# Both matrices of an MLP in seven block products for eight, the first one completed before the second begins

## What is computed

```
def sq_relu_mlp(h, w1, w2):
    return jnp.square(jax.nn.relu(h @ w1)) @ w2
```

## Time and profile before

| | us |
|---|---|
| median of 3 runs | 1949.92 (1949.31 to 1952.12) |
| the profiled execution | 1952.2 |
| its span, first to last instruction | 1950.1 |
| PE busy | 1911.8 (98%), 8432 matmuls |
| DVE busy | 1542.7 (79%) |
| ACT busy | 819.8 (42%) |
| POOL busy | 575.8 (30%) |

### The profile page before, as it was taken

How to read it: one execution, slowest core, us unless ns; L and a number is a source line. 1 busy time by engine, 2 the same in 40 slices (tenths; PEclk the granted TensorE clock), 3 DMA queues, 4 the chain that set the end, 5 groups by cost and what they waited for, 6 DMA issues and landing times.

```text
span 1950.1 us, 22012 instructions
## 1 busy us (share of the span) xinstructions
PE 1911.8 (98%) x8432; PEld 1567.0 (80%) x8432; DVE 1542.7 (79%) x1677; ACT 819.8 (42%) x1011; POOL 575.8 (30%) x261
## 2 busy tenths in 40 slices
PE   7899999999999999999999999999999999999997
PEld 4678888878887878888888888888888888888886
DVE  7989999978898898768677686776867768677683
ACT  5455555553423344434334343343434434344343
POOL 0009999930000022322222222222222232222301
PEclk9999999999999999999999999999999999999998
DMA  9973222237797714222442224432244332342332
GB/s 389 401 273 109 100 94 95 99 149 292 299 408 281 295 67 172 102 97 102 150 151 100 98 98 147 145 114 97 98 139 146 109 108 97 135 152 103 109 130 86
DMA packets 83342, 308.87 MB, mean 158 GB/s; under 512 B 6705, under 2 KB 6961, under 8 KB 58673
## 3 DMA queue, kind: packets, MB, share of 16 engines
q1 hardware_dynamic: 83250, 307.64, 42.9%
HBM read 299.23 MB, written 8.39 MB: 158 GB/s over the span
## 4 chain that ended last, share of the span: by engine, by line
PE 84%; DVE 12%; issue 1%; ACT 1%; DMA 1%; SPq 1%; POOL 0%; POOLq 0%; DVEq 0%; ACTq 0%
PE ps L555 14%; PE ps L759 10%; PE ps L757 10%; PE ps L763 10%; PE ps L781 9%; PE ps L783 9%; PE ps L788 9%; PE ps L560 7%; DVE raw L1245 2%; DVE adar L1245 2%; DVE wlo L1267 2%; DVE ps L1341 1%; DMA raw<-w 1%; PE ps L821 1%; PE ps L822 1%
## 5 line engine op out<-in xcount | busy, mean ns | idle before, releaser
L1766 POOL TENSOR_TENSOR raw<-raw 128x1024 f32<-128x1024 f32 x116 | 315.3, 2718 | 1139.5 <-DVE wlo L1550 1136.1
L1550 DVE TENSOR_TENSOR wlo<-raw,whi 128x1024 fp32r<-128x1024 f32 x210 | 333.1, 1587 | 258.2 <-ACT whi L1108 258.0
L1108 ACT ACTIVATE whi<-raw 128x1024 fp32r<-128x1024 f32 x210 | 221.9, 1060 | 473.6 <-PE ps L763 327.7
L757 PE MATMUL ps<-hhi,whi 128*128 128x512 f32 x896 | 348.5, 389 | 0.0
L759 PE MATMUL ps<-hlo,whi 128*128 128x512 f32 x896 | 348.5, 389 | 0.0
L781 PE MATMUL ps<-whi,dhi 128*128 128x512 f32 x840 | 327.0, 389 | 1.5 <-DVE xb L1627 1.5
L783 PE MATMUL ps<-whi,dlo 128*128 128x512 f32 x840 | 326.8, 389 | 0.0
L555 PE MATMUL ps<-hlo,whi 128*128 128x512 f32 (+1 forms) x896 | 300.4, 390 | 7.1 <-DVE hlo L1251 7.1
L555 PE MATMUL ps<-hhi,whi 128*128 128x512 f32 (+1 forms) x896 | 301.2, 391 | 2.6 <-ACT hhi L1078 0.8
L1633 DVE TENSOR_TENSOR xb<-xb,ps 128x1024 f32<-128x1024 f32 x202 | 245.7, 1217 | 40.3 <-PE ps L788 40.3
L1341 DVE SCALAR_TENSOR_TENSOR ps<-xb,pr,ps 128x502 f32<-128x502 f32 (+22 forms) x358 | 230.8, 730 | 3.2 <-ACT ps L948 3.2
(11 more groups left out here) (192 smaller groups left out, 2122.1 us busy)
## 6 DMA issues: line engine op xcount, KB each, us to landing
raw<-w SPq DMA_DIRECT2D x112, 1024.0 KB, 6.7
raw<-w SPq DMA_DIRECT2D x128, 512.0 KB, 6.3
adar<-ada SPq DMA_DIRECT2D x36, 1024.0 KB, 7.4
raw<-ada SPq DMA_DIRECT2D x36, 1024.0 KB, 7.1
adaq<-ada SPq DMA_DIRECT2D x64, 256.0 KB, 3.3
xb<-xT SPq DMA_DIRECT2D x8, 1024.0 KB, 8.5
ada_h<-ada SPq DMA_DIRECT2D x4, 1024.0 KB, 17.9
ada_l<-ada SPq DMA_DIRECT2D x4, 1024.0 KB, 20.6
```

Source lines behind the costliest of these rows:

```text
L757: pe.matmul(ps[:, bank, :], tile, ch(hhi, 8 * h + k), start=h == 0 and k == 0, stop=False, skip_group_check=True)
L1550: dve.tensor_tensor(product_ring(wlo, n), quarter_tiles(g, OPERAND[i]), f(product_ring(whi, n)), ALU.subtract).then_inc(s_lo, 1)
L1766: pool.tensor_tensor(quarter(g, out), quarter(g, of), quarter(g, by), ALU.subtract).then_inc(t_done, 1)
```

## The change

**First matrix.** Tiles 0 to 7 stay as they are. Tiles 8 to 11 are made plainly (`direct_unit`, eight slots). Tiles 12 to 63 are made by 26 sets (`SETS`). A set is two row tiles of the hidden layer against the two halves of the channels and the two halves of the tokens: a 2 x 2 by 2 x 2 block product, in seven products (`product1`) of 24 matmuls whose moving operand has 256 columns (`HT`). The four sums of weight blocks of a set are made in place in `raw` by DVE (`sum1`), the four differences of `h` once, by POOL into `xb` and from there split into `t_upper` and `t_lower`. Three accumulators of a set leave PSUM on the way: `leave` on ACT copies three of them, and `c22`, `c12`, `c11` on DVE and `c21` on ACT make the four corners of the set.

**Forms.** All forms of 15 sub-blocks go through three staging buffers into a DRAM tensor (`fd`, `store_form` on SP), 105 of 512 KB each.

**Second matrix.** It begins when the first is complete. Its arithmetic is that of before, but two sub-blocks at a time are added in PSUM, in `GROUPS` (8): group 0 has one sub-block, groups 1 to 7 have two. So a half of the outputs of one group (`k`, `p`) has 14 slots and seven `take`s. The forms are read from DRAM into `hhi` and `hlo`, whose `h` is no longer needed, by DMAs that POOL issues (`load_form`, `load_sub`: 28 DMAs of 256 KB for a group), between its `term`s. The last sub-block is multiplied plainly as before, from forms in `hhi` and `hlo`.

**Smaller edits.** `x1` is parked in DRAM earlier; the last norm's input lies in other buffers (`fx`); `h2_hi` on ACT writes the full `h` first and then copies its high part; before the second product of the convolution PE warms up with 6 matmuls of 512 columns in place of 11 of 256; the order of PSUM banks at the end is another.

```diff
-PAIRS = 7
-GATES = (2, 2, 2, 2, 2, 3, 3)
 SUB = 4
 NSUB = FF // P // SUB
 HALF = U // 2
 RING = 4
 PROD = 7
 FORM = SUB // 2 * (T // 2)
-SLOTS_U = 2 * 2
-LAST_PAIR = 2 * NSUB - 3
-LAST_SLOTS = 2 * PROD + (LAST_PAIR - 1) * (SLOTS_U + PROD)
+HT = T // 2
+STAGES = 3
+DIRECT = 2 * SUB
+FIRST_SET = 3
+SETS = 2 * (NSUB - FIRST_SET)
+FORMS = (NSUB - 1) * PROD
+GROUPS = NSUB // 2
+W2 = DIRECT + SETS * PROD
+LAST_SLOTS = W2 + (NSUB - 1) * 2 * PROD
+GATE_AT = (1, 3, 5, 7, 10)
...
+        fd = nc.dram_tensor("forms", (FORMS, P, 2 * FORM), F32).ap()
...
+        WEIGHT1 = ((0, 0), (1, 0), (0, 0), (1, 0), (0, 0), (0, 1), (1, 1))
+        SUM1 = (None, 1, 2, 3, 4, None, None)
+        T_OF = (None, 1, 2, None, 3, None, 4)
+
+        def act1(x, k):
+
+            two, first = KC // 2 + k, bass.ds
+            if x in (0, 5, 3):
+                at = (two if x else k) * T + (HT if x == 3 else 0)
+                return hhi[:, first(at, HT)], hlo[:, first(at, HT)]
+            if x == 1:
+                return t_upper[:, k * HT:(k + 1) * HT], t_lower[:, k * T:k * T + HT]
+            if x == 2:
+                return t_upper[:, U + k * HT:U + (k + 1) * HT], t_lower[:, two * T + HT:two * T + T]
+            if x == 4:
+                return hhi[:, k * T + HT:k * T + T], t_lower[:, k * T + HT:k * T + T]
+            return hlo[:, k * T + HT:k * T + T], t_lower[:, two * T:two * T + HT]
...
+        MAKE = (2, 6, 5, 0, 3, 4, 1)
+        OF_SUM = {2: (0, 1), 5: (1, 2), 3: (0, 3), 1: (1, 4)}
+        PLAIN = {6: (1, 1), 0: (0, 0), 4: (0, 1)}
...
+            def store_form(n):
+
+                sp.wait_ge(form_lo, n + 1)
+                b, i = n // PROD, MAKE[n % PROD]
+                sp.dma_start(fd[b * PROD + i], stage(n % STAGES)).then_inc(form_out[n % STAGES], 16)
...
+            def product1(z, x):
+
+                n = slot1(z, x)
+                out = ps[:, bank1(z, (0, 2, 0, 2, 0, 1, 0)[x]), 0:HT]
+                fresh = x in (0, 1, 5)
                 pe.wait_ge(s_hi, n + 1)
...
+                if z == 0 and T_OF[x]:
+                    pe.wait_ge(t_lo, T_OF[x])
+                if x == 0:
+                    if z < 2:
+                        pe.wait_ge(tile_relu, (8, 12)[z])
+                    else:
+                        pe.wait_ge(c21_done, z - 1)
+                elif x == 1 and z >= 2:
+                    pe.wait_ge(c12_done, z - 1)
+                elif x == 5 and z >= 2:
+                    pe.wait_ge(c11_done, z - 1)
+                elif x == 2:
+                    pe.wait_ge(m1_out, z + 1)
+                elif x == 3:
+                    pe.wait_ge(m5_out, z + 1)
+                elif x == 4:
+                    pe.wait_ge(u2_out, z + 1)
+                elif x == 6:
+                    pe.wait_ge(c22_done, z + 1)
+                for k in range(8):
+                    tile = ring(whi, n)[:, k * P:(k + 1) * P]
+                    hi, lo = act1(x, k)
+                    pe.matmul(out, tile, hi, start=fresh and k == 0, stop=False, skip_group_check=True)
+                    pe.matmul(out, tile, lo, start=False, stop=False, skip_group_check=True)
+                pe.wait_ge(s_lo, n + 1)
+                for k in range(8):
+                    last = pe.matmul(out, ring(wlo, n)[:, k * P:(k + 1) * P], act1(x, k)[0], start=False, stop=False,
+                                     skip_group_check=True)
+                last.then_inc(s_mm, 1)
...
+            for v in range(SUB):
+                direct_unit(v)
+            for z in range(SETS):
+                for x in range(PROD):
+                    product1(z, x)
+            for k in range(GROUPS):
+                for p in range(2):
+                    for i in range(PROD):
+                        for a in range(subs(k)):
+                            product2(k, p, i, a)
...
+            def leave(z, kind, dest, n, done, x):
+
+                act.wait_ge(s_mm, slot1(z, x) + 1)
+                act.activation(small1(dest), ps[:, bank1(z, kind), 0:HT], ACT.Copy).then_inc(done, 1)
...
+            def sum1(z, n):
+
+                out, of, by = (((1, 0), (1, 0), (1, 1)), ((0, 0), (1, 0), (0, 0)),
+                               ((1, 0), (0, 1), (0, 0)), ((0, 0), (1, 1), (0, 0)))[n - 1]
+                if n == 1:
+                    dve.wait_ge(row_in[z % 2 * 2 + 1], 16 * (z // 2 + 1))
                 else:
...
+                    dve.wait_ge(s_sum, 4 * z + n - 1)
+                    dve.wait_ge(s_lo, slot1(z, n - 2) + 1)
+                dve.tensor_tensor(block1(z, *out), block1(z, *of), block1(z, *by), ALU.add if n == 1 else ALU.subtract
+                                   ).then_inc(s_sum, 1)
...
+            def c22(z):
+
+                b = z // 2 + 2
+                dve.wait_ge(m5_out, z + 1)
+                dve.wait_ge(s_mm, slot1(z, 4) + 1)
+                if z % 2 == 0:
+                    dve.wait_ge(form_lo, PROD * b + 2)
+                    dve.wait_ge(form_sum, 4 * b + 1)
+                dve.tensor_tensor(ch(hid, 2 + z % 2, HT, HT), ps[:, bank1(z, 0), 0:HT], small1(2), ALU.add
+                                  ).then_inc(c22_done, 1)
...
+            for z in range(SETS):
+                b = z // 2 + 2
+                for x in range(PROD):
+                    if x == 4:
+                        c22(z)
+                    if x == (3 if z % 2 else 6):
+                        c12(z)
+                    if z % 2 and x == 1:
+                        c11(z - 1)
+                    if z % 2 and x == 5:
+                        c11(z)
+                    ahead(z, x)
+                    if z == 0 and x == 0:
+                        t_low(4)
+                    if z % 2 == 0:
+                        if x == 0:
+                            form_add(b, 1)
+                        if x == 3:
+                            form_add(b, 2)
+                        if x == 4:
+                            form_add(b, 3)
+                        if x in (1, 2, 3, 5, 6):
+                            form_rest(PROD * b + (1, 2, 3, 5, 6).index(x))
+                    elif x == 0:
+                        form_add(b, 4)
+                        form_rest(PROD * b + 5)
+                    elif x == 2:
+                        form_rest(PROD * b + 6)
...
+            gate = 0
+            for k in range(GROUPS):
+                for p in range(2):
+                    for j in range(subs(k) * PROD):
+                        i, a = j // subs(k), j % subs(k)
+                        if a == subs(k) - 1:
+                            take(k, p, i)
+                        slot_lo(slot2(k, p, i, a) + RING)
...
-            for g in range(1, LAST_PAIR + 1):
-                for n in range(1, 5):
-                    term(g, n)
...
+            def load_form(k, i):
+
+                if k >= GROUPS:
+                    return
+                pool.wait_ge(s_mm, slot2(k - 1, 1, i, subs(k - 1) - 1) + 1)
+                for a in range(2):
+                    load_sub(2 * k - 1 + a, i, a)
+
+            for n in range(STAGES):
+                pool.wait_ge(form_out[n], 16 * 3)
+            for i in range(PROD):
+                if i in (0, 2, 4, 6):
+                    pool.wait_ge(s_mm, slot1(SETS - 1, (0, 3, 5, 6)[i // 2]) + 1)
+                load_sub(0, i, 0)
+            for k in range(GROUPS):
+                for p in range(2):
+                    for n in range(1, 5):
+                        for a in range(subs(k)):
+                            term(set_of(k, p, a), n, k, p, a)
+                        if p == 0 and k and n == 2:
+                            load_form(k, 5)
+                        if p == 0 and k and n == 3:
+                            load_form(k, 6)
+                        if p == 1 and n == 3:
+                            load_form(k + 1, 0)
+                            load_form(k + 1, 1)
+                    if p == 1:
+                        if k == 0:
+                            for n in range(STAGES):
+                                pool.wait_ge(form_out[n], 16 * (FORMS // STAGES))
+                        for i in (2, 3, 4):
+                            load_form(k + 1, i)
```

More of the change, by code:

```diff
@@ L111, in trunk_kernel @@
             ada_l = sb("ada_l", [P, 2, U], scope=first)
-        with ExitStack() as last:
-            xf = sb("xf", [P, KC * T], scope=last)
         hlo = sb("hlo", [P, KC * T], F32R)
@@ new lines, in t_parts, with bank1, stage @@
+        def t_parts(n):
+            src, low = (quadrants(buf[:])[:, (0, 1, 0, 1)[n - 1], :, (0, 1, 1, 0)[n - 1], :] for buf in (xb, t_lower))
+            if n < 3:
+                return src, t_upper[:, (n - 1) * U:n * U].rearrange("p (k n) -> p k n", n=HT), low
+            return src, quadrants((hhi if n == 3 else hlo)[:])[:, 0, :, 1, :], low
+        def bank1(z, kind):
+            return (0 if z % 2 else 4) + kind
+        def stage(n):
+            return wide[:, 2 * U + n * 2 * FORM:2 * U + (n + 1) * 2 * FORM]
@@ new lines, in _ @@
+            load_direct(2)
```

(58 more changed lines are left out.)

843 lines of the change are left out of this document (475 added, 368 removed).

## The result

The changed kernel takes 2021.09 us (median of 4 runs, 2019.85 to 2024.05) where the kernel before takes 1949.62: a ratio of 1.0366, 95% interval 1.0348 to 1.0384. It is slower by 3.7%, outside the range of 1880 to 2005. The profiled execution has a span of 2018.4 us, 68.3 more than before.

What follows compares the result with a forecast made beforehand. PE's matmuls were taken to set the time. Terms -70.7 + 12 + 1 + 4 + 2 + 28 = -23.7 took the profiled 1952.2 to 1928.5, less 2.3 for the median: 1926 us, 8-in-10 range 1880 to 2005.

Steps and rivals of the forecast that it cites:

- matmuls of the first matrix: PE in the sets: 4368 matmuls of 256 columns at 0.1133 us replace 2496 of 512 at 0.2266: -70.7 us.
- `c22` in even sets: First matrix: product 6 waits for `c22` on DVE 0.9 us, 13 times: +12 us (0 to 25).
- ahead of and in the first eight tiles: One more copy on ACT, 1.06 us, ahead of the MLP's first tile: +1 us (0 to 1).
- group 0, from the first matrix into the second: Between the matrices, POOL's first `term` comes behind loads waiting for PE's last product: +4 us (2 to 12).
- groups 1 to 7: Second matrix: 14 halves of 40.1 us, 2.0 over PE, as `term`s and DVE hinder each other: +28 us (0 to 70).
- last sub-block and tail: The last sub-block starts with forms just loaded: +2 us (0 to 5).
- the bound I had named: First matrix: 256-column matmuls at 0.120 us, 13 ns paid per matmul, making the matmul term -41 us.
- So I add up: 8 x 3.15 = 25.2 ...: Second matrix: eight `term`s, then remaining low parts, `take`s and gate parts, make a half 38.6 to 43.1 us; 40.1 taken.
- SP's 0.86 makes 37.2, just under PE: Second matrix: POOL's `term`s plus 14 load issues at SP's price of 0.86 us stay under PE's 38.1 per half.
- rival two: POOL's queue bounds the second matrix, deciding if an issue costs above 1.06 us; about 2011 us at 1.5; chance 0.23.
- Small edits: Extra ACT copy +1 us; `t`'s sums on POOL beside the direct tiles, stores of forms and warm-up matmuls 0.
- The sign: Whole kernel: faster 0.62, the same 0.07, slower 0.31.

Runs made afterwards that it cites:

- Experiment 6: Changed kernel with the rest of form 2 behind `c22` on DVE in even sets, not ahead of it: 2008.39 us.
- experiment 4: Changed kernel with loads of forms issued for groups 0 and 1 only, POOL keeping all its `term`s (sum not the reference's): 1980.68 us.
- Experiment 1: Changed kernel with POOL issuing the loads of form 5 after term 3, not after term 2, in first halves: 2004.79 us.
- experiment 2: Changed kernel with the gate parts of a half at slots 1, 4, 7, 9, 12, not 1, 3, 5, 7, 10: 2013.32 us.
- experiment 5: Changed kernel with the eight `term`s of a half done by DVE, POOL only issuing the loads of forms: 1944.87 us.
- experiment 10: Changed kernel with `term`s on DVE, rest of form 2 behind `c22`, and, in its last version, gate parts at slots 0, 2, 4, 6, 8: 1922.99 us.
- experiment 7: Changed kernel with each of the four stores of `x1` writing 256 KB for 1 MB (final sum from other values): 2014.78 us.

## Why the prediction was wrong

The sum of its terms against what the stages took (us; spans, 1950.1 and 2018.4):

| term | forecast | measured |
|---|---|---|
| matmuls of the first matrix | -70.7 | -41.4 |
| `c22` in even sets | +12 | +12.4 |
| ahead of and in the first eight tiles | +1 | +12.3 |
| start of the first set | 0 | +6.2 |
| group 0, from the first matrix into the second | +4 | +9.4 |
| groups 1 to 7 | +28 | +74.7 |
| last sub-block and tail | +2 | -1.1 |
| idle time of PE in the MLP before, now gone | 0 | -4.2 |
| sum | -23.7 | +68.3 |

**The matmul was mis-sized.** The step was "I take 0.1133, the nearest". In PE's timeline of the sets (changed kernel), 24 matmuls take 901.48 - 898.60 = 2.88 us, 0.1200 each:

```profile
897.63 1.12 PE L955 MATMUL ps<-t_upper,wlo 128*128 128x256 f32 x8
898.60 0.28 PE L951 MATMUL ps<-t_upper,whi 128*128 128x256 f32 x1
...
900.51 1.12 PE L955 MATMUL ps<-t_upper,wlo 128*128 128x256 f32 x8
901.48 0.28 PE L951 MATMUL ps<-hhi,whi 128*128 128x256 f32 x1
```

That is the bound I had named: 13.3 ns per matmul beside the columns, paid by twice as many. 4368 x 0.1200 = 524.2, so 41.4 saved and not 70.7. An eighth fewer columns in all (4368 x 256 for 2496 x 512) is 7% less time. The Trainium skill's formula (TensorE: Matmul & The Clock Gate, Back-to-back issue gap), 109 ns, is farther off than my value.

**The wait of `c22` was right** in place, count and size: 12 waits that make an even set 0.95 longer, 0.9 forecast, and one in the first set. Experiment 6 removes the 12 by the very cause that was argued. That the size fits so well is partly luck: products 4 and 5 cover 2 x 2.88 = 5.76 us and not 5.44, so the stretch ahead of `c22` is some 6.7 us long (an estimate, 5.76 + 0.95) and not 6.35. One figure of the working is a slip: seven forms in a pair's 38.1 us are one every 5.4 us, not 9.5. Nothing hung on it, for sets without the wait of `c22` take 20.16, their matmuls alone.

**The largest step, the second matrix, was right in one part and failed in the other.** "So I add up: 8 x 3.15 = 25.2 ..." gave 40.1 for what `term`s and low parts do to each other, and experiment 4, which leaves that alone, gives 40.3: 2.2 us a half, 31 of the 74.7, for a forecast of 28. What failed is "SP's 0.86 makes 37.2, just under PE", by which the loads of forms cost nothing; the other 44 us come with them. An issue costs even less, 0.72, so over a group's two halves POOL's sum is on average 25.2 + 14 x 0.72 = 35.3 of 38.1: by its sum POOL does not bind, and rival two, priced by a sum, has the right side, by luck nearly the right time (2011 for 2021) and the wrong reason. A half needs its `term` 3 about 15 us after its start (six slots less ACT's 1.06), with hardly any slack, and in a first half three things that each fit on average stand ahead of it in line: slow `term`s, loads of forms, and low parts that DVE gives late because a gate load is late. Experiment 1 shows the second, experiment 2 the third, experiments 4 and 5 the first. How the 44 us divide between place in the queue, traffic and late gate loads stays open; with the `term`s on DVE and the gate loads ahead of the weights on SP, experiment 10 shows, the loads of forms cost PE nothing.

The Trainium skill's lock (SBUF — State Buffer, Who interferes with whom) agrees with experiment 5: with POOL's `term`s gone, DVE does more operations in less busy time. Its sum, 38.0 of 38.1, was no forecast of the half, for it leaves out who waits for whom.

**Small edits cost 18.5 us that I put at 1.** 6.9 us are the earlier stores of x1, which I had not priced at all: they fall into a stretch where DVE's reductions use each load as it lands (experiment 7). Of the 6.9, 3.3 pass before the norm's matmuls begin (596.11 for 592.83), and the rest in them: they run at a granted clock of 0.50 after a wait of PE of 4.0 us, where the kernel before had 1.00 after one of 0.9. 5.4 lie in the first eight tiles, where PE waits 2.8 us for a high part of `h` and runs on at a lower clock (0.98 over the stage). No run tries their cause, but the timelines of POOL, DVE and PE point to it:

```profile
638.86 6.59 POOL L2110 TENSOR_TENSOR xb<-xb 128x2048 f32<-128x2048 f32 x1 [230.20 <-DVE hlo L1755]
640.91 6.69 DVE L1509 SCALAR_TENSOR_TENSOR raw<-raw,csb 128x2048 f32<-128x2048 f32 x1
652.28 2.73 PE L715 MATMUL ps<-hhi,whi 128*128 x8 [2.75 <-ACT hhi L1280]
```

The first of `t`'s sums on POOL, which I had put at 0, runs here and not beside the direct tiles. A reduction on DVE that takes 2.29 us elsewhere takes 6.69 beside it, and the parts of `h` that ACT's high part needs stand behind it on DVE. 6.2 lie at the first set: PE waits 3.8 us for ACT's copy of an accumulator (L1407), and in ACT's timeline two high parts of `t` (L1355) stand ahead of it, where I had looked only at POOL:

```profile
744.70 1.92 ACT L1355 ACTIVATE hhi<-xb 128x2048 fp32r<-128x2048 f32 x1
746.50 1.91 ACT L1355 ACTIVATE hlo<-xb 128x2048 fp32r<-128x2048 f32 x1
...
750.85 0.39 ACT L1407 ACTIVATE wide<-ps 128x256 f32<-128x256 f32 x1
```

That this is the cause was not tried. Group 0, behind the first matrix, costs 9.4 and not 4: the first `term` began at 1286.3, 2 us into it, as I had said, and three of them then took 8.2. With the `term`s on DVE (experiment 5) its two halves take 19.07 and 19.04, so all of the 9.4 goes with `term`s on POOL.

**The chances.** The sign was given 0.31. The rival that holds the result was named, but its deciding point (the price of an issue) was the wrong one to watch.

## What to carry to other kernels

Cost a queue not by its sum but by the moment at which each item is wanted, with everything that stands ahead of it in line: here a queue with room for 7% more work held PE up every half. An operation that two engines can do belongs on the one whose own operations it would otherwise slow down, if that one has room: eight terms at 1.13 us on VectorE cost less than VectorE's waiting beside eight at 2.4 to 3.2 on GpSimd. And where a block product halves the columns, price the matmul with its fixed part from two sizes before counting the saving; with a weight tile for each matmul it ends at 112 ns here.
